# Key up-projections from rounded halves, and four gate rows in other places

## The reference

```python
mod = c_act @ w_ada[l] + b_ada[l]
shift, scale, gate = jnp.split(mod, 3, axis=-1)
h = rms_norm(x) * (1.0 + scale[:, None, :]) + shift[:, None, :]
proj = h @ w_in[l]
xr, gr, qc, kvc, kr, ga = jnp.split(proj, split_points(IN_SPLITS), axis=-1)
...
q = (rms_norm(q_comp, q_a_norm) @ w_uq).reshape(B, S, MLA_HEADS, QK_NOPE + QK_ROPE)
kv = (rms_norm(kv_comp, kv_a_norm) @ w_ukv).reshape(B, S, MLA_HEADS, QK_NOPE + V_HEAD)
q_nope, q_pe = q[..., :QK_NOPE], q[..., QK_NOPE:]
k_nope, v = kv[..., :QK_NOPE], kv[..., QK_NOPE:]
...
y_rnn = rg_lru_branch(...) * jax.nn.silu(gr)
y_att = mla_branch(...) * jax.nn.silu(ga)
y = jnp.concatenate([y_rnn, y_att], axis=-1) @ w_out[l]
x = x + gate[:, None, :] * y
```

## Time and profile before

| | us |
|---|---|
| median of 3 runs | 2674.0 |
| the three runs | 2673.74 to 2674.05 |
| the profiled execution's own time | 2673.43 |
| its span | 2671.6 |
| TensorE busy | 2660.4 |
| VectorE busy | 2017.1 |
| ScalarE busy | 1230.4 |

### The profile page before, as it was taken

One profiled execution on the slowest core, in us unless ns is written; L12 is line 12 of the kernel. 1 busy time (PEld: TensorE's weight loads), 2 busy tenths in 40 slices (PEclk: granted clock), 3 DMA queues, 4 the chain that ended last, 5 costly groups with the idle time before them and its releaser, 6 DMA issues.

```text
span 2671.6 us, 44754 instructions
## 1 busy us (share of the span) xinstructions
PE 2660.4 (100%) x15576; PEld 2341.7 (88%) x15576; DVE 2017.1 (75%) x2628; ACT 1230.4 (46%) x1568; POOL 5.7 (0%) x12
## 2 busy tenths in 40 slices
PE   9999999999999999999999999999999999999999
PEld 7888988888888888888888888888888888888888
DVE  6678887778787788657877766698878775688865
ACT  2025655555554444444444543466544444444443
POOL 0000000000000000000000000000000000000000
DMA  9998566555556666666666566654666666666664
GB/s 348 359 334 266 184 196 192 167 164 170 169 162 190 193 191 192 196 194 194 191 189 196 185 202 190 186 158 130 200 188 190 189 195 195 189 194 194 195 201 154
DMA packets 706502, 532.40 MB, mean 199 GB/s; under 512 B 32301, under 2 KB 694639, under 8 KB 706031
## 3 DMA queue, kind: packets, MB, share of 16 engines
q1 hardware_dynamic: 702448, 525.83, 64.0%
q10 hardware_dynamic: 3967, 5.40, 0.6%
HBM read 525.90 MB, written 4.19 MB: 198 GB/s over the span
## 4 chain that ended last, share of the span: by engine, by line
PE 95%; DVE 3%; ACT 1%; issue 0%; DMA 0%; DVEq 0%; SPq 0%; ACTq 0%
PE acc L765 81%; PE acc L891 2%; PE turned L903 1%; PE sums L903 1%; PE acc L903 1%; PE acc L929 1%; PE acc L930 1%; PE acc L931 1%; PE mixed L1045 1%; PE sums L1304 1%; DVE pro_ada L2070 1%; DVE wr L1997 0%; PE scores L1297 0%; PE sums L803 0%; DVE xc L2266 0%
## 5 line engine op out<-in xcount | busy, mean ns | idle before, releaser
L765 PE MATMUL acc<-stream,wr 128*128 128x512 f32 (+1 forms) x7680 | 1328.4, 333 | 0.4 <-DVE wr L1997 0.4
L765 PEld LDWEIGHTS acc<-stream,wr 128*128 128x128 f32 x7680 | 1158.8, 188 | 156.2 <-issue 3.8
L1997 DVE TENSOR_TENSOR wr<-raw,wr 128x1024 fp32r<-128x1024 f32 x832 | 998.6, 1222 | 316.5 <-ACT wr L1480 306.7
L1480 ACT ACTIVATE wr<-raw 128x1024 fp32r<-128x1024 f32 x832 | 871.1, 1058 | 695.2 <-PE acc L765 674.5
L765 PE MATMUL acc<-ys,wr 128*128 128x512 f32 (+1 forms) x4264 | 732.5, 332 | 0.9 <-DVE wr L1997 0.9
L765 PEld LDWEIGHTS acc<-ys,wr 128*128 128x128 f32 x4264 | 642.9, 188 | 85.2 <-DVE wr L1997 1.5
L765 PE MATMUL acc<-wr,stream 128*128 128x512 f32 (+1 forms) x1024 | 182.7, 338 | 0.0
L765 PEld LDWEIGHTS acc<-wr,stream 128*128 128x128 f32 x1024 | 157.0, 188 | 22.5 <-issue 0.5
L1881 ACT ACTIVATE ffn_cv<-ffn_cv 128x256 f32<-128x256 f32 x88 | 36.9, 419 | 245.1 <-DVE ffn_cv L2659 245.1
L2007 DVE TENSOR_REDUCE ffn_ug<-acc 128x512 f32<-128x1024 f32 x88 | 107.8, 1225 | 35.2 <-PE acc L765 35.2
L2030 DVE TENSOR_TENSOR ys<-tmp,ys 128x256 f32 (+3 forms) x108 | 51.2, 474 | 76.0 <-ACT ys L1486 73.4
(11 more groups left out here) (371 smaller groups left out, 1809.3 us busy)
## 6 DMA issues: line engine op xcount, KB each, us to landing
raw<-in_ffn_w_up SPq DMA_DIRECT2D x704, 256.0 KB
raw<-in_ffn_w_down SPq DMA_DIRECT2D x160, 512.0 KB
raw<-in_a_w_qkv SPq DMA_DIRECT2D x96, 512.0 KB
raw<-in_b_w_kv SPq DMA_DIRECT2D x64, 512.0 KB
aring<-in_w_ada SPq DMA_DIRECT2D x96, 256.0 KB, 6.7
w<-in_w_in SPq DMA_DIRECT2D x48, 512.0 KB
raw<-in_w_ada SPq DMA_DIRECT2D x32, 512.0 KB, 5.8
raw<-in_w_out SPq DMA_DIRECT2D x32, 512.0 KB
```

Source lines behind the costliest of these rows:

```text
L765: mm = pe.matmul(*ops, start=first and ops is wide, stop=last and ops is wide)
L1480: f(half_of(0, s), raw[:, s, :], ACT.Copy)\
L1997: tt(half_of(1, s), raw[:, s, :], half_of(0, s), ALU.subtract).then_inc(T.unit_split[s].sem, 1)
```

## The change

`N_UQ` goes from 6 to 10, so U6 to U9 are made from rounded halves too: `kvx_high` is a copy on ScalarE at n = 2 behind that iteration's `high()`, `kvx_low` a subtraction on VectorE at n = 4 behind `low()`, and TensorE waits for it before U6. ScalarE makes highs at n = 1 to 6 and VectorE lows at n = 1 to 7. Four gate rows leave the iterations n = 5 (one), 6 (one) and 7 (two): one goes in front of the queries' norm (3 instead of 2), one to n = 14, one to the first round with `rnn_gate`, and one to head 7. The load of row 6 moves from behind U3 to behind the last XR unit. `gate_sums(1)` moves from slot 18 to slot 19, where it stands behind the last head's output. Left out of the diff are two lists that get the names of the semaphores `kv_high` and `kv_low`.

```diff
--- before.py
+++ after.py
@@ -103,7 +103,7 @@
 
 ONE_FREE = [max(users_of(ONE_SPAN[n], n) + [n - ONE_RING + 1, 0]) for n in range(ONE_UNITS)]
 HIGH_FREE = [max(users_of(HIGH_SPAN[n], n)) if n >= GR_AT else 0 for n in range(ONE_UNITS)]
-N_UQ = 6
+N_UQ = 10
 for _n in range(U_AT + 1, U_AT + N_UQ):
     HIGH_FREE[_n] = XR_AT + 1 + _n - U_AT if _n < U_AT + 4 else _n - 2
 
...
@@ -423,6 +423,8 @@
         p1 = [o(f"p{e}", [3 * P]) for e in range(2)]
         pT1 = [o(f"pT{e}", [3 * P]) for e in range(2)]
         qn, kn = o("qn", [8, TOK]), o("kn", [8, TOK])
+        kvx_high = nc.alloc_sbuf_tensor_at("kvx_high", [P, LT, TOK], F32R, offset=o.at)
+        kvx_low = S_high
         v1 = o("v", [2, HEADS * V_DIM])
         qpe = o("qpe", [4, TOK])
         ssq = sb("ssq", [2, TOK])
@@ -636,7 +638,7 @@
                 gate_load()
             for i in range(4):
                 quarter_load(i, 3)
-                if i in (1, 2):
+                if i in (1, 2, 3):
                     gate_load()
             for n, (what, g) in enumerate(U_PAIRS):
                 if what in ("nope", "rope"):
@@ -647,7 +649,7 @@
                              "v": (2, NOPE, NOPE + V_DIM)}[what]
                 one_load(*((lambda n, j=j: unit_tiles(n)[:, :, j * (256 // per):(j + 1) * (256 // per)],
                             w[:, :, per * g + j, e0:e1]) for j in range(per)))
-                if n in (3, 4, 5, 6, 10, 11, 12, 13):
+                if n in (4, 5, 6, 10, 11, 12, 13):
                     gate_load()
                 if n == 6:
                     recurrent_load()
@@ -911,15 +913,15 @@
                 pe.wait_ge(*F.low_out.next())
                 return high_tiles(n), low_tiles(n)
 
-            def query_tiles(out):
+            def up_tiles(out, x_high, x_low):
 
                 high, low = split_unit()
                 for j in range(2):
                     for k in range(UK):
                         cols = slice(j * P, (j + 1) * P)
-                        pe.matmul(out(j), high[:, k, cols], qx_high[:, k, :], start=k == 0, stop=False)
-                        pe.matmul(out(j), high[:, k, cols], qx_low[:, k, :], start=False, stop=False)
-                        mm = pe.matmul(out(j), low[:, k, cols], qx_high[:, k, :], start=False, stop=k == UK - 1)
+                        pe.matmul(out(j), high[:, k, cols], x_high[:, k, :], start=k == 0, stop=False)
+                        pe.matmul(out(j), high[:, k, cols], x_low[:, k, :], start=False, stop=False)
+                        mm = pe.matmul(out(j), low[:, k, cols], x_high[:, k, :], start=False, stop=k == UK - 1)
                 mm.then_inc(F.w1_used.sem, 1)
 
             def three_products(out, high, low, j, k, k0, first, last):
@@ -1103,8 +1105,12 @@
                 if n == 0:
                     pe.wait_ge(F.latent_low.sem, 1)
                 out = halves(take(U_BANK[n], read=(F.heads_out.sem, 2 + n) if what != "v" else None))
-                if n < N_UQ:
-                    query_tiles(out)
+                if n == 6:
+                    pe.wait_ge(F.kv_low.sem, 1)
+                if n < 6:
+                    up_tiles(out, qx_high, qx_low)
+                elif n < N_UQ:
+                    up_tiles(out, kvx_high, kvx_low)
                 else:
                     two_tiles(out, kvx, 0, tokens_out=what == "v")
                 if n >= 1:
@@ -1126,7 +1132,7 @@
                     latent_out((at - 5) // 4)
                 if slot == 0:
                     gate_sums(0)
-                if slot == 18:
+                if slot == 19:
                     gate_sums(1)
 
             F.mixed_read.n = 2
@@ -1639,9 +1645,12 @@
                 else:
                     f(v1[:, :, 256 * g:256 * g + 256], bank(U_BANK[n]).rearrange("p (m c) -> p m c", m=2), ACT.Copy)\
                         .then_inc(F.bank_read[U_BANK[n]].sem, 1)
-                if n in (1, 2):
+                if 1 <= n <= 6:
                     high()
                 if n == 2:
+                    act.wait_ge(F.bank_read[3].sem, 1)
+                    f(flat(kvx_high[:, :, :]), flat(kvx[:, :, :]), ACT.Copy).then_inc(F.kv_high.sem, 1)
+                if n == 6:
                     high_units[0] = GR_AT
             gates(3)
             high()
@@ -2328,7 +2337,7 @@
             low(4)
             dve.wait_ge(F.w1_used.sem, XR_AT)
             xm_lows(3).then_inc(F.last_lows.sem, 1)
-            gate_row(2)
+            gate_row(3)
             lora_out("q")
             rnn_in(0)
             dve.wait_ge(F.latent_high.sem, 1)
@@ -2346,13 +2355,16 @@
             for n in range(N_U + 2):
                 if n == 2 or n == 4 or n == 5:
                     conv({2: 1, 4: 2, 5: 3}[n])
-                if 1 <= n <= 3:
+                if 1 <= n <= 7:
                     low()
-                if n == 3:
+                if n == 4:
+                    dve.wait_ge(F.kv_high.sem, 1)
+                    tt(flat(kvx_low[:, :, :]), flat(kvx[:, :, :]), flat(kvx_high[:, :, :]), ALU.subtract).then_inc(F.kv_low.sem, 1)
+                if n == 7:
                     low_units[0] = GR_AT
                 if N_U - 1 <= n <= N_U:
                     low()
-                gate_row({5: 1, 6: 1, 7: 2, 8: 2, 9: 2, 10: 3, 11: 3, 12: 3, 13: 2}.get(n, 0))
+                gate_row({8: 2, 9: 2, 10: 3, 11: 3, 12: 3, 13: 2, 14: 1}.get(n, 0))
                 if 0 <= n - 1 and n - 1 < N_U and U_PAIRS[n - 1][0] != "v":
                     head_out(n - 1)
                 if 0 <= n - 2 < N_U and U_PAIRS[n - 2][0] == "rope":
@@ -2435,8 +2447,7 @@
             F.scores_ready.n, F.scores_read.n = 8, 8
             for i in range(3):
                 low()
-                if i:
-                    gate_row()
+                gate_row()
                 rnn_gate(i)
             for hd in range(8):
                 it = hd // 2
@@ -2461,7 +2472,7 @@
                         low()
                 else:
                     low(2)
-                if hd in (0, 1, 2, 4, 6):
+                if hd in (0, 1, 2, 4, 6, 7):
                     gate_row()
             split_units(1)
             rnn_lo(2)
```

More of the change, by code:

```diff
@@ L254 @@
      "one_scores_ready", "one_scores_read", "one_mixed_ready", "one_mixed_read", "one_heads_out", "rgw_zeroed", "pack_in",
-     "ada_product", "high_ready", "high_out", "low_out", "h_kept", "h_back", "last_lows", "latent_high", "latent_low"]
+     "ada_product", "high_ready", "high_out", "low_out", "h_kept", "h_back", "last_lows", "latent_high", "latent_low", "kv_high", "kv_low"]
     + [f"ada_in{s}" for s in range(ADA_RING)] + [f"w1_in{s}" for s in range(ONE_RING)]
@@ L267, in __init__ @@
          self.pack_in, self.ada_product, self.high_ready, self.high_out, self.low_out,
-         self.h_kept, self.h_back, self.last_lows, self.latent_high, self.latent_low, *slots) = [Tally(s) for s in sems]
+         self.h_kept, self.h_back, self.last_lows, self.latent_high, self.latent_low, self.kv_high, self.kv_low, *slots) = [Tally(s) for s in sems]
         self.ada_in, slots = slots[:ADA_RING], slots[ADA_RING:]
```

## The result

| | before | after |
|---|---|---|
| median of 6 runs, us | 2673.87 (2673.27 to 2674.32) | 2684.32 (2683.60 to 2684.71) |
| ratio to before, 95% interval | | 1.0039 (1.0029 to 1.0049) |
| profiled execution: time, span, us | 2673.43, 2671.6 | 2684.71, 2682.8 |
| first product of w_out starts, us | 350.85 | 362.06 |
| DMA busy share, 243 to 266 us | 1.00 | 0.93 |

The direction was right, the size too small: 2680.4 forecast, range up to 2684.0. All of the 11.2 us of the span are lost before the output product starts. low(GA0) is VectorE's low half of unit GA0, at its start.

The account below looks back on a forecast made before the run. The prediction took TensorE to bound the kernel (busy 2660.4 of 2671.6 us); 4.7 (ring) + 2.0 (heads) - 0.3 (end) = 6.4 us later, by the median of 2674.0 gave 2680.4 us, range 2673.0 to 2684.0.

Parts of the forecast that it names:

- TensorE's saving: Key up-projections U6 to U9: each takes 2.82 us instead of 3.45, so four units save 2.5 us.
- VectorE's operations spend it: Up-projections: VectorE's five new operations delay U6 and the first rope turn; U10 starts 0.5 us later, the whole saving spent.
- The ring: SyncE's queue of gate-row loads: load 11 waits for row 7, GR3 lands late, GA0's low is 4.7 us late (3.4 to 6.5).
- The heads: Head loop: GA4 and GA5 stand behind loads 30 and 31, which wait for moved rows; +2.0 us (0 to 3.2).
- 288.7 + s: Head loop: forecast issue time of load 30, with s for the 4.7 us of the ring.
- Nothing more is given back in the loop: Head loop: ScalarE and VectorE wait for each other, not for TensorE, so none of the lateness is recovered.
- the rival in which the heads give it back: Head loop: GA0 is late but ScalarE and VectorE have unseen slack; 2677 to 2679 us, chance 0.10.
- The one in which the end starves: Output product: last row delays its second and third unit, w_out's fourth load lands late; 2681.7 to 2684 us, chance 0.10.
- The row at head 7 costs nothing: Last head: the moved row takes VectorE 1.3 us before the output product's second unit; cost taken as 0 (up to 1.3).
- - 0.3: End of the heads: TensorE can start unit GA15 earlier, since gate_sums(1) now stands behind it; -0.3 us.
- the case's own bounds: Whole kernel: the main forecast, chance 0.50, reaches from 2677.1 to 2684.7 us with its terms' bounds.
- 1.3 for the last head: Last head: upper bound on the delay of the output product from the row moved there, taken as 0.

Follow-up runs that it names:

- b2: The changed kernel with convolutions, gate rows and loads spread over other places, gate_sums(1) at its old slot and load 31 behind GA8; 2671.53 us, ratio 0.9991.
- b3: b2 without the rounding: the keys' up-projections in fp32 as in the kernel before; 2674.41 us, ratio 1.0002.
- e5: The changed kernel with loads 30 and 31 issued behind GA8 and GA9 instead of in front of GA4 and GA5; 2679.27 us, ratio 1.0020.
- e8: The changed kernel with GR3's load issued ahead of loads 22 to 25 instead of behind them; 2679.27 us, ratio 1.0024.
- e2: The kernel before with the gate rows, row 6's load and gate_sums(1) moved as in the change, without the rounding; 2680.36 us, ratio 1.0024.
- e3: The changed kernel with idle products nobody reads in TensorE's two waits, for kvx_low and the first rope turn; 2684.04 us, ratio 1.0038.
- e9: The changed kernel with the load orders of e5 and e8 both at once; 2675.64 us, ratio 1.0007.
- e10: e9 with the idle products of e3 in TensorE's two waits; 2675.28 us, ratio 1.0006.
- e4: The changed kernel with the loads of U12, U13, GR0 and GR1 issued ahead of load 11; 2680.20 us, ratio 1.0024.
- e1: The changed kernel with every gate row, its load and gate_sums(1) back in their old places, rounding kept; 2677.14 us, ratio 1.0014.

## Why the prediction was right in kind and too small

- **TensorE's saving, 2.5 us:** right. U10 starts 2.6 us apart in b2 and b3. The price of a unit, 2.82, is in U9's and its sum's period of 3.68 (242.41 to 246.09). The estimate from the four passes that the Trainium skill ("FP8 and Floating Point Precision", TensorE Precision Notes) gives for true FP32 was 3.5 us, which no run bears out.
- **VectorE's operations spend it:** right to 0.2 us where they act: U6 at 226.70 (226.5), the first turn at 232.47 (232.5). After it the clock, which the prediction did not look at, moved U10 to 246.95, not 245.4. In the profiled executions of e5 and e8, with the same wait of 1.85 us, the clock stayed at 1.00; e5 had the sum behind the first turn at 236.23, and U10 at 245.31 and load 11 at 242.70, both as forecast.
- **The ring, +4.7 us: the step that failed first.** The mechanism held: GR3's load waits behind row 21, as named. The size did not: low(GA0) was 7.4 us late. The forecast took 32.3 us from load 11 to GR3 by bytes (1 us, which stands in no row, and 31.3 at the 353 GB/s of the earlier trace rows) and put 1.3 on top. It knew that a row of the kernel before had come 3.0 us later than such a sum, but gave half of that to the small pieces of the U loads, which no run shows. Measured from load 11 to GR3's high are 34.6 us in the changed kernel (244.33 to 278.92), 34.8 in e2, 35.4 in e3 and 35.8 in e5 (242.70 to 278.50): 2.3 to 3.5 beyond the sum by bytes where 1.3 was allowed. In e5, where load 11 went at the forecast moment, this step alone is 2.2 us short. In the changed kernel it is 1.0, and the other 1.6 is load 11's own lateness, which came with the clock; without the fall GR3's high was only 0.4 to 0.6 us sooner there (e5, e3), so the clock's 1.6 is not to be added to what the ring costs.

The rate was too high: 353 GB/s was that of the fullest 23 us. Over the kernel before's whole stretch from load 10 on it was 332, and behind load 11 in the changed kernel 333:

```profile
229.50:266.00 36.50, 36.18 (x155) 29.34 (x155) 30.79 (x31) 18.87 (x34) 0.00 (x0) 1.00 0.98 332
...
244.00:279.00 35.00, 35.00 (x210) 31.37 (x208) 25.96 (x24) 20.55 (x41) 0.00 (x0) 1.00 0.95 333
```

At 333 GB/s the 31.3 us are 33.2, which is 1.9 of the 2.3 to 3.5. Why the rate is below 353 is read, not tested: each load of a row waits for a row four earlier, which waits for its own data, and loads 12 to 14 took 5.7 to 8.9 us to land in the changed kernel and in e3, e5, e8, e9 and e10. No run has a ring of another depth. (The forecast also calls the queue full until about 286; the share before was 0.66 from 280 to 284 us, but no term hangs on it.)

- **The heads, +2.0 us: the second term that was too small; +3.9.** Load 30 went at 296.10, which is the forecast 288.7 + s exactly. GA4's data came 5.5 us after, GA5's 5.6 us after load 31 (305.10 to 310.67); 4.6 had been taken for both. Twice 0.9 to 1.0 is the difference. In the forecast's own steps: 2.2 at GA4 (taken 1.3), 2.3 at GA5 (1.3), and then 0.6 back (0.7 back and 0.1 lost). e5 takes both waits away, and 5.0 us go with them.
- **Nothing more is given back in the loop:** right; the lows of GA7, GA9, GA13 and GA15 are all 11.3 us late, so the rival in which the heads give it back is false. The one in which the end starves is false too: lateness is 11.3 at low(GA15) and 11.2 at the output product. The row at head 7 costs nothing, as taken.
- **The sum:** 4.7 + 2.0 - 0.3 = 6.4 forecast, 7.4 + 3.9 - 0.1 = 11.2 measured.
- **The range:** it was cut at 2684.0 and the measured time is 2684.3, although the case's own bounds reached 2684.7. Both terms also came out above their own upper ends (7.4 against 6.5, 3.9 against 3.2). The sum of the bounds hid that, because it also allowed 1.3 for the last head, which was not needed.

Open: how much of an earlier load 11 arrives behind it. In single profiled executions 1.4 us of it became 0.2 at row 14 (e3 against the changed kernel), and 1.7 us became 1.1 (e10 against e9); but in e8, whose loads up to there are those of e9 and whose clock stayed at 1.00, 1.7 us stayed 1.8, and low(GA0) was 2.0 us earlier than in e9. Load 14 took 7.4 to 8.9 us to land in these executions, so a part may be chance. What the medians show is that keeping the clock up was worth 0.3 us (e3) and 0.4 us (e10), neither of them clear of noise.

## What to carry to other kernels

Where one queue issues both the loads of a ring and loads that wait for nothing, the ring's order is a price on everything behind it: list, for each load that an engine will wait for, the last slot it stands behind, and put it ahead of that slot before any of the ring's work is moved. Price such a load by its landing as measured over the whole full stretch, not by bytes over the rate of the best part of it. And an operation that is moved off a crowded engine should not leave the transfers idle in the meantime: here 20 us of stillness were followed by 35 of nearly full engines.

## What was not expected of the hardware

- The clock fell to the lower level for some 3 us after a wait of 1.84 us in the profiled executions of the changed kernel, e4 and e9 (1.85), but not in those of e5 and e8 with the same wait, nor in e1 with one of 3.04 us. Three matmuls of 256 columns then took 0.64 us instead of 0.35. With idle products in the waits (e3, e10) it stayed at 1.00 in the up-projections. In the heads it fell after waits of 2.52 us (the changed kernel), 2.53 (e3), 1.88 (e2) and 1.90 (e8), but not after 2.52 in e5.
- In the heads a gate unit's load of 512 KB landed 5.1 and 5.2 us after its own issue, at DMA shares of 0.56 (296 to 302 us) and 0.80 (305 to 311 us). In the changed kernel's full stretch loads 12, 13 and 14, one after the other, took 5.8, 6.7 and 7.4 us.
- The same load 14 took 7.4 us in the changed kernel and 8.2 in e9, whose loads up to there are the same: single landings differ by as much as some of the effects above.
